# Between the stages of a transformer kernel: residual rows turned over by token tile through a diagonal of roots

## The reference, cut to what matters

```python
def rms_norm(x, g):
    y = x * lax.rsqrt(jnp.mean(x * x, -1, keepdims=True) + EPS)
    return y * g

h = x
for i in range(2):
    a = rms_norm(h, norm_g[i, 0])
    a = mla_mixer(a, ...) if i == 0 else diff_mixer(a, ...)
    h = h + rms_norm(a, norm_g[i, 1])
    f = conv_ffn(rms_norm(h, norm_g[i, 2]), ...)     # up to 2 x 2816, conv of 3, gelu * val, down
    h = h + rms_norm(f, norm_g[i, 3])
x = h
# second block: q, k, v of two attentions, an indexer (qi, ki, wi) and two gates from one product
p = rms_norm(x, g_mix) @ w_in
x = x + mixed(p) @ w_out
x = x + hier_moe(rms_norm(x, g_ffn), ...)            # 32 experts, two of them for a token
return rms_norm(x, g_final)
```

## Time and profile before

| | |
|---|---|
| median of three runs | 1344.09 us |
| the profiled execution | 1345.34 us |
| its span, from first to last instruction | 1343.5 us |
| PE busy | 1282.8 us, 95% |
| POOL, ACT, DVE busy | 573.2, 548.0, 509.6 us |
| DMA | 341.22 MB, mean 254 GB/s |

### The profile page before, as it was taken

One profiled execution on the slowest core, in us unless ns is written; L12 is line 12 of the kernel. 1 busy time (PEld: TensorE's weight loads), 2 busy tenths in 40 slices (PEclk: granted clock), 3 DMA queues, 4 the chain that ended last, 5 costly groups with the idle time before them and its releaser, 6 DMA issues.

```text
span 1343.5 us, 20032 instructions
## 1 busy us (share of the span) xinstructions
PE 1282.8 (95%) x7959; PEld 954.6 (71%) x7959; DVE 509.6 (38%) x1303; ACT 548.0 (41%) x853; POOL 573.2 (43%) x136
## 2 busy tenths in 40 slices
PE   6999999999998899999999999999999999999996
PEld 6867999998987799999878888854444444454442
DVE  2434444445265454444657453421111111121112
ACT  4654555556477465555543664311111111111112
POOL 4722788885944188888567855200000000000001
PEclk9999999999999999999999999999999999999998
DMA  8731666664633266664446444599999999999994
GB/s 270 235 94 63 182 195 188 190 199 144 220 126 95 63 203 196 196 188 165 149 165 203 159 137 161 230 421 426 427 428 428 429 428 429 429 429 428 429 423 189
DMA packets 156933, 341.22 MB, mean 254 GB/s; under 512 B 8537, under 2 KB 119482, under 8 KB 144314
## 3 DMA queue, kind: packets, MB, share of 16 engines
q1 hardware_dynamic: 156858, 340.18, 68.1%
HBM read 339.10 MB, written 1.05 MB: 253 GB/s over the span
## 4 chain that ended last, share of the span: by engine, by line
PE 75%; DMA 13%; ACT 4%; DVE 4%; POOL 2%; issue 1%; SPq 0%; ACTq 0%; DVEq 0%
PE bank L669 16%; PE bank L671 15%; PE bank L670 15%; PE bank L1237 11%; DMA xspare<-in_w 6%; DMA ring<-in_w 6%; PE bank L1262 5%; PE bank L1187 3%; PE bank L768 2%; POOL parts L621 2%; PE bank L679 1%; PE bank L1217 1%; ACT parts L1305 1%; PE bank L1105 1%; PE bank L1121 1%
## 5 line engine op out<-in xcount | busy, mean ns | idle before, releaser
L621 POOL TENSOR_TENSOR parts<-raw,parts 128x2048 fp32r<-128x2048 f32 (+4 forms) x128 | 568.0, 4466 | 290.2 <-ACT parts L1305 290.2
L669 PE MATMUL bank<-xh,parts 128*128 128x256 f32 x1032 | 288.0, 279 | 6.0 <-POOL parts L621 4.0
L670 PE MATMUL bank<-xl,parts 128*128 128x256 f32 x1032 | 285.9, 277 | 0.0
L671 PE MATMUL bank<-xh,parts 128*128 128x256 f32 x1032 | 285.8, 277 | 0.0
L1305 ACT ACTIVATE parts<-raw 128x2048 fp32r<-128x2048 f32 (+4 forms) x128 | 236.1, 1853 | 23.4 <-PE bank L669 8.5
L1237 PE MATMUL bank<-ring,room 128*64 128x512 f32 x768 | 226.1, 594 | 7.1 <-DMA ring<-in_w 4.5
L644 POOL TENSOR_TENSOR xn<-h,gpost 128x512 f32<-128x512 f32 x4 | 4.9, 1270 | 474.7 <-DVE h L2258 474.7
L669 PEld LDWEIGHTS bank<-xh,parts 128*128 128x128 f32 x1032 | 194.2, 188 | 12.6 <-POOL parts L621 4.8
L670 PEld LDWEIGHTS bank<-xl,parts 128*128 128x128 f32 x1032 | 193.8, 188 | 0.8
L671 PEld LDWEIGHTS bank<-xh,parts 128*128 128x128 f32 x1032 | 193.9, 188 | 0.0
L1237 PEld LDWEIGHTS bank<-ring,room 128*64 128x64 f32 x768 | 72.5, 137 | 111.4 <-issue 111.4
(11 more groups left out here) (255 smaller groups left out, 1858.9 us busy)
## 6 DMA issues: line engine op xcount, KB each, us to landing
ring<-in_w SPq DMA_DIRECT2D x67, 2048.0 KB, 22.9
raw<-in_ffn_w_up SPq DMA_DIRECT2D x88, 512.0 KB, 4.9
room<-in_w SPq DMA_DIRECT2D x12, 2048.0 KB, 20.3
raw<-in_ffn_w_down SPq DMA_DIRECT2D x44, 512.0 KB, 3.9
xspare<-in_w SPq DMA_DIRECT2D x11, 2048.0 KB, 26.6
raw<-in_w_in SPq DMA_DIRECT2D x40, 512.0 KB, 4.1
raw<-in_diff_w_qkv SPq DMA_DIRECT2D x24, 512.0 KB, 4.6
ring<-in_w SPq DMA_DIRECT2D x10, 1024.0 KB, 24.8
```

The costliest lines, as they stand in the source:

```text
L621: pool.tensor_tensor(low[:, p % PARTS, 0:n], raw[:, p % RING, 0:n], high[:, p % PARTS, 0:n], ALU.subtract).then_inc(low_ready, 1)
L669: first = pe.matmul(out_, a[0], b[0], start=start, stop=False)
L670: pe.matmul(out_, a[0], b[1], start=False, stop=False)
L671: return first, pe.matmul(out_, a[1], b[0], start=False, stop=stop)
```

## The change

At x1, x2 and x3:

- `turned_over` takes the place of `post`. It works by token tile: both halves of tile 0 (L1842), its sum (L1849), half of it (L1824), its root (L1832, L1833), its residual (L1858), and then the same of tile 1, with the second half of tile 1 between its sum and its root. ACT gives a guess per tile, and waits for the sum of tile 0 ahead of the squares of the third bank.
- `normed` is gone. `spread_roots` writes, for each token tile, the identity times the column of roots (`spread_r`, a 128 x 128 block, L1877).
- `h_transposed` multiplies the block of `h` (as the stationary operand) by that diagonal (L715), which turns the block over and scales it by the roots at once, eight products for a token tile. A bank now holds two feature tiles of all 256 tokens.
- The norm weights lie in `gcol`, one column per feature tile, and are the scale of ACT's copy to `xh` (`high_chunks`, 8 of 128 x 256, L1398) and of DVE's `xl` (`low_chunks`, 8 of 128 x 256, L1800). They arrive as 32 rows of 512 bytes, and are transposed with other parameters in the first stage.
- The first product of the next stage waits for the low parts of the first bank (feature tiles 0 and 1) alone, the later ones for theirs as they come to them.
- `keep_clock` runs 16 products in place of 32.

At x4 the same `turned_over`; the rows of `h` are transposed as they are (L717), the weights are applied in `high_chunks` and `low_chunks` too, and `keep_clock` runs 4 products. The groups of `qi` that follow are placed in banks 0 to 3.

In both FFNs the last piece of the down product computes all of token tile 0 (banks 4 and 5) ahead of token tile 1 (banks 6 and 7). The four 512 KB transfers of norm weights at these sites and SP's waits for their readers are gone.

The diff, with the removed functions left out (they stand in the kernel above) and the repeated places cut:

```diff
+            def h_transposed(name, site, scaled):
+                b = [begin(G[name] + q) for q in range(4)]
+                for t in range(NT):
+                    if scaled:
+                        pe.wait_ge(spread_ready, 2 * (site - 1) + t + 1)
+                    else:
+                        pe.wait_ge(h_ready, 2 * (site - 1) + t + 1)
+                    for k in range(KT):
+                        at = S * (k % 2) + P * t
+                        dst, src = b[k // 2][:, at:at + P], h[:, t, P * k:P * k + P]
+                        if scaled:
+                            ins = pe.matmul(dst, src, spread_r[:, t], start=True, stop=True)
+                        else:
+                            ins = pe.transpose(dst, src, ident)
+                        if t == 0 and k == 0:
+                            behind(ins)
+                        if t and k % 2:
+                            end(ins, G[name] + k // 2)
+                late.extend([(2 * q, G[name] + q) for q in range(4)])
             def keep_clock(n, b, x=xh):
...
             late = []
             def k_tile(k):
-                if k == 4:
-                    while late:
-                        moved(pe, late.pop(0))
+                while late and late[0][0] <= k:
+                    moved(pe, late.pop(0)[1])
             def by_token(g0, p0, x, k_counts, widths, order=None, k_from=0, k_all=None, x_from=0):
...
-                                                     [y[:, (j + x) % 4, t * P:t * P + P] for y in (hh, hl)],
-                                                     [y[:, x, 512 * hf:512 * hf + 512] for y in w],
-                                                     start and x == 0, stop and x == 1)
-                                behind(first)
-                                if stop and x == 1:
-                                    ins.then_inc(ffn_full, 1)
+                    each = [(x, t, hf) for x in range(2) for t in range(NT) for hf in range(2)]
+                    if stop:
+                        each = [(x, t, hf) for t in range(NT) for x in range(2) for hf in range(2)]
+                    for i, (x, t, hf) in enumerate(each):
+                        if not any(x == y for y, _, _ in each[:i]):
+                            pe.wait_ge(hid_ready, n + (n0 + 1 + x))
+                        first, ins = product(bank[4 + 2 * t + hf][:, :],
+                                             [y[:, (j + x) % 4, t * P:t * P + P] for y in (hh, hl)],
+                                             [y[:, x, 512 * hf:512 * hf + 512] for y in w],
+                                             start and x == 0, stop and x == 1)
+                        behind(first)
+                        if stop and x == 1:
+                            ins.then_inc(ffn_full, 1)
...
             ffn(1)
-            keep_clock(WAIT, bank[3])
-            x_transposed("x4", 4)
+            keep_clock(WAIT // 4, bank[3])
+            h_transposed("x4", 4, False)
...
                               bank[BANK[g]][:, 0:n * P].rearrange("p (a b) -> p a b", b=P), scale)
+            def high_chunks(name, site):
+                for k in range(KT):
+                    g = G[name] + k // 2
+                    full(act, g)
+                    act.activation(xh[:, k, :], bank[BANK[g]][:, S * (k % 2):S * (k % 2) + S], ACT.Copy,
+                                   scale=gain_of(site, k)).then_inc(x_high, 1)
             def tiles(g, dst, t, n, scale=1.0):
...
                 for n, (b, wait) in enumerate(banks):
                     wait(act)
-                    if n == 0:
+                    squares(st[:, 2 + n:3 + n], bank[b][:, :], view(6400 + 512 * n, 512), post_squares)
+                    if n % 2:
+                        t = n // 2
                         outs_done[0] += 1
-                    squares(st[:, 2 + n:3 + n], bank[b][:, :], view(6400 + 512 * n, 512), post_squares)
-                act.wait_ge(sums_ready, outs_done[0])
-                guess(st[:, 16:18], st[:, 18:20], D)
+                        act.wait_ge(sums_ready, outs_done[0])
+                        guess(st[:, 16 + t:17 + t], st[:, 18 + t:19 + t], D)
...
+            def low_chunks(name, site):
+                for k in range(KT):
+                    g = G[name] + k // 2
+                    x_parts[0] += 1
+                    dve.wait_ge(x_high, x_parts[0] + (1 - k % 2))
+                    ins = dve.scalar_tensor_tensor(xl[:, k, :], bank[BANK[g]][:, S * (k % 2):S * (k % 2) + S],
+                                                   gain_of(site, k), xh[:, k, :], ALU.mult, ALU.subtract)
+                    if k % 2:
+                        ins.then_inc(bank_moved[BANK[g]], 1)
...
+                scales(site)
+            def half_of(t, src):
+                steps[0] += 1
+                dve.tensor_scalar(st[:, 32 + t:33 + t], src, -0.5 / D, -0.5 * EPS, ALU.mult, ALU.add).then_inc(vec, 1)
+            def root_of(t, y):
+                guesses[0] += 1
+                dve.wait_ge(guessed, guesses[0])
+                dve.wait_ge(vec, steps[0])
+                a = st[:, 48 + t:49 + t]
+                link(dve.tensor_scalar(a, y, y, st[:, 32 + t:33 + t], ALU.mult, ALU.mult))
+                link(dve.tensor_scalar(y, a, 1.5, y, ALU.add, ALU.mult))
+            def turned_over(site, banks, ring_groups):
+                def gained_half(t, hf):
+                    b = banks[2 * t + hf]
+                    dve.wait_ge(post_squares, 4 * site + 2 * t + hf + 1)
+                    x = slice(512 * hf, 512 * hf + 512)
+                    ins = dve.tensor_tensor(xn[:, t, x], bank[b][:, :], gpost[:, x], ALU.mult)
                     ins.then_inc(bank_moved[b] if ring_groups else vec, 1)
+                    if not ring_groups:
+                        steps[0] += 1
+                def summed(t):
+                    dve.wait_ge(post_squares, 4 * site + 2 * t + 2)
+                    dve.tensor_tensor(st[:, 18 + t:19 + t], st[:, 2 + 2 * t:3 + 2 * t], st[:, 3 + 2 * t:4 + 2 * t],
+                                      ALU.add).then_inc(sums_ready, 1)
+                    dve.wait_ge(sums_ready, 2 * site + t + 1)
+                    half_of(t, st[:, 18 + t:19 + t])
+                def residual(t):
+                    root_of(t, st[:, 16 + t:17 + t])
+                    for g in (ring_groups or [])[2 * t:2 * t + 2]:
+                        moved(dve, g)
                     dve.scalar_tensor_tensor(h[:, t, :], xn[:, t, :], st[:, 16 + t:17 + t], h[:, t, :],
                                              ALU.mult, ALU.add).then_inc(h_ready, 1)
+                dve.wait_ge(gpost_here, 16 * (site + 1))
+                gained_half(0, 0)
+                gained_half(0, 1)
+                summed(0)
+                residual(0)
+                gained_half(1, 0)
+                summed(1)
+                gained_half(1, 1)
+                residual(1)
+            def spread_roots(site):
+                for t in range(NT):
...
+            low_chunks("x4", 4)
+            scales(4)
             rows = [G["qi"] + 2 * c + t for c in range(2) for t in range(NT)]
```

## The result

The changed kernel took 1356.27 us (median of 10 runs, 1352.07 to 1361.07), the kernel before 1345.74 us (10 runs, 1343.32 to 1350.77). The ratio is 1.0072, interval [1.0054, 1.0091]: it is slower, by some 10 us. The forecast was 1341.1 us, faster by 3.0, with a range of 1336.8 to 1345.0.

What follows compares the result with a forecast made beforehand. PE was taken to bound the kernel, so only its waits at the four sites could give time. Terms 3.1 (x1 and x3), -1.5 (x2) and +1.4 (x4) made 3.0 us: 1341.1 us, range 1336.8 to 1345.0.

Steps and rivals of the forecast that it cites:

- At nothing: Side effects counted as free: dropped transfers, `gcol` copy (0.2 us if DVE were late), down-piece order, later shifts of pieces.
- the fall: Granted clock dropping to its lower level behind PE's waits; 1.7 us each, counted as 1.4 at x2, 1.1 at x4.
- Slower: Rival, chance 0.07: clock stays low through the turning over, 1.7 us a stretch; eight stretches would make 1352 us.
- x1 and x3: Sites ahead of the two FFNs: 0.63 us gained up to R, 0.93 behind it; 1.56 each, 3.1 together.
- R: End of the second `h` residual at a site; forecast 0.63 us earlier at x1 and x3, 1.05 later at x2.
- x2: Site behind FFN 0: 0.93 us gained behind R, 1.05 lost ahead, 1.4 lost to the clock; -1.5 in all.
- the lock: Port pair shared by DVE and POOL: tile 0's sum at x2 waits 1.4 us for POOL's split.
- x4: Site behind FFN 1: first product 2.55 us earlier, less 1.1 for a fall of the clock; +1.4.
- The clock: PE waits of 2.2 us at x1 and x3 bring no fall; 3.8 us at x2 brings one, costing 1.4.
- The sum: All four sites: 3.1 - 1.5 + 1.4 = 3.0 us gained, the median going from 1344.09 to 1341.1 us.

Runs made afterwards that it cites:

- e2: The changed kernel, unchanged, run again beside the kernel before on one chip: 1359.73 us, ratio 1.0097.
- e4: The changed kernel with `gcol` allocated last, so every other tile lies where the kernel before has it: 1347.34 us, ratio 1.0021.
- e1: The kernel before, unchanged, run again: 1345.35 us, ratio 0.9996.
- e7: e4 with `keep_clock` of 22, 30, 22 and 20 products at the four sites in place of 16, 16, 16 and 4: 1342.27 us, ratio 0.9958.
- e8: e4 with the sum of a tile's two halves (L1849) as addition of a per-partition scalar instead of two blocks: 1345.21 us.
- e15: e4 with `keep_clock` of 20 products instead of 4 at x4 alone: 1344.28 us, ratio 0.9992.
- e16: e4 with `keep_clock` of 30 products instead of 16 at x2 alone: 1345.58 us, ratio 0.9994.
- e3: The kernel before with an unused tile of 128 bytes a partition where the changed kernel has `gcol`: 1363.69 us, ratio 1.0134.
- e11: e4 with the edits of e7 and e8 together: 1340.74 us, ratio 0.9970.

## Why the prediction was wrong

It failed in the step "At nothing". There `gcol` was counted as a copy of 0.2 us, and its 128 bytes were not counted. The whole sum rests on products that step as in the trace of before (0.12); I never asked whether the change leaves that true. This term is 12.4 us by the medians of e2 and e4 and 10.2 by their ratios, over three times everything else that was forecast, and no rival had it.

A second step failed with it: the fall was priced too low and counted only at the sites. With the place restored the forecast of 3.0 us faster still does not hold, since e4 is 1.9 to 2.8 us slower. Leaving out the one at the very end, the clock is low for eight stretches of 3.4 us in e4's trace and for three in that of before: one each at x2 and x4, as forecast, and net three more behind them, which were counted at nothing. By the forecast's own figures five more stretches make 5.55 - 5 x 1.7 = -3.0, slower by 3.0 us. This agrees with e4, but it rests on one trace of each, and the count changes between executions (e1's trace has two). The rival *Slower* had this price and this count (slower from the fourth stretch on), but not the reason: e7 shows that the pause lets the clock fall, and not the work in pieces. The trace of the changed kernel itself has nine such stretches. So the sites and the clock together left the kernel 2 to 3 us slower, and the place did the rest: 12.4 of the 14.3 us by which e2 lay above the kernel before.

By its own steps:

- *x1 and x3*: R came 4.3 us behind the start of `keep_clock` (125.65 - 121.36), where 5.45 stood before and 4.8 was forecast; the first product 5.6 us behind R, where 6.5 stood and 5.35 was forecast. Together 2.1 us at each, 1.8 forecast. Of the 0.2 us by which the first product came later than R+5.35, the sum itself has a part: it allows 0.2 for each engine's start, but from R+4.5 two low parts of 0.43 already make 5.36, so that none is left for DVE's. A diagonal product is two instructions and 0.24 us, 3.81 for sixteen: as taken from the earlier trace rows.
- *x2*: the lock is there as forecast, and the sum ends with POOL's split. Its size is less: R came 5.7 us behind the start of `keep_clock`, 0.2 later than before and not 1.05, since POOL's split ended 0.03 behind that start (312.00 + 9.19 against 321.16) and not 0.53, and the steps from there to R took 5.6 us and not 5.9. In e4, where the split does end 0.53 behind, R is 0.7 later. Here the Trainium skill (SBUF — State Buffer, "SBUF: two separate sides") speaks of a lock for the whole instruction, against VectorE operations with two SBUF inputs. The 1.32, the 1.76 of e4 (it ends with POOL's split, at 313.75 and 313.74) and e8's 0.20 and 1.70 agree with it.
- *x4*: the first product 2.55 earlier was forecast, 2.9 was measured. The lock did not touch this sum: POOL's split was over 0.04 behind its start, and it took 0.15. In e4 it took 0.47.
- *The clock*: falls at x2 and x4 and none at x1 and x3 were forecast, and so it was. The size was off: one stretch each, 2.5 us together, was forecast. The changed kernel shows two at each, e4 one at each and two more at 696; without those of e4 the medians are 4.9 us lower (3.1 in e15 and 1.8 in e16). A fall behind POOL's first split of FFN 0 came too (146 us, the row above). It is not the change's: the wait is 1.92 us there as in the kernel before, and e3, which has no changed site, fell at the same place behind the same 1.92, while the second trace of the changed kernel did not.
- *The sum*: without any fall the sites would give 5.55 us, and 0.7 less with e7's longer `keep_clock` at x4 (7.75 us to the first product and not 7.02). e7 measured 3.3 us by the medians and 5.7 by the ratio, between 2.7 and 8.6: it agrees. So what the sites give at full clock was right. What the clock takes was not, and the place of the tiles was left out.

## What to carry to other kernels

A change is also what it does to the addresses of everything allocated behind it: put a new tile last, and compare the count of PE's instructions in windows where nothing was changed, since a busy share of 100% hides a slower step. Take more than one window and execution: FFN 1 of one and the same kernel counted 736 and 715. When PE's filler work is cut, leave it long enough to reach the instruction that PE waits for; read the granted clock in the windows behind, as the price is paid by products of the next stage.

## What the runs showed of the hardware

- A TensorE instruction whose stationary and moving operand are fp32 parts in SBUF mostly stepped 0.113 us (256 columns) where the distance of the two tiles had the remainder 192 in 256 bytes, and 0.118 at 64 (with short stretches of 0.113), 0.119 on average at 128 and 0.120 at 0. For 512 columns it was 0.229 at 192, 0.233 at 64, 0.232 at 128 and 0.228 at 0. Kernels with `xh` off 192 took 0.7 to 1.3% longer than the kernel before, at a granted clock of 1.00 in the window compared.
- At 192 both steps of the 256-column instruction occur: about five slow ones behind each block of down products, and long turns that differ between executions. In e1 such a turn began behind a wait of PE of 2.12 us at 476.6 and lasted for 975 instructions; the other trace of the same kernel kept 0.113 behind the same wait. What sets them is open.
- A DVE addition of two 128x1 blocks took 1.32 and 1.76 us beside a POOL instruction, ending with it, 0.15 alone, and 0.20 beside POOL with one of them as a per-partition scalar.
- Behind 16 products of `keep_clock` the granted clock fell where PE paused 3.0, 3.5 and 2.4 us at x2, not where it paused 1.6 to 1.8 at x1 and x3. In e7 and e11, with more of these products and pauses of 0.44 us or less ahead of the diagonals, it fell at none of the four sites.
